# The split products of a two-model transformer kernel with their moving operand and their PSUM columns taken in descending order

## What is computed

```
h = modulate(x, g_norm1, sh1, sc1)
proj = h @ w_in                                  # 1024 x 5024
y = g_mla*(o_mla @ w_br_mla) + g_gqa*(o_gqa @ w_br_gqa) + g_four*(o_four @ w_four)
x = x + gt1 * (y @ w_o)
u = modulate(x, g_norm2, sh2, sc2) @ w_up        # 1024 x 5632
u = conv3(u) + conv_b
a, v = split(u, 2); x = x + gt2 * ((silu(a) * v) @ w_down)
...
gate, up = split(x @ wi, 2); x = x + (silu(gate) * up) @ wo
```

## Time and profile before

| | |
|---|---|
| median of 3 runs | 2618.41 us (2617.87 to 2620.92) |
| span of the profiled execution | 2618.2 us |
| PE busy | 2498.0 us, 95% |
| PEld busy | 2204.9 us, 84% |
| DVE busy | 1609.7 us, 61% |
| ACT busy | 1333.9 us, 51% |
| POOL busy | 585.6 us, 22% |
| mean granted TensorE clock | 0.985 of full |
| HBM traffic | 171 GB/s |

### The profile page before, as it was taken

The page is one execution under the profiler, slowest core; times in us unless marked ns, Lnnn a source line. Parts: engine busy times, 40 slices in busy tenths (PEclk is TensorE's granted clock), DMA queues, the critical chain, the costliest instruction groups (busy, mean ns, idle before and its releaser), DMA issues. The chain is left out here.

```text
span 2618.2 us, 46369 instructions
## 1 busy us (share of the span) xinstructions
PE 2498.0 (95%) x17358; PEld 2204.9 (84%) x17358; DVE 1609.7 (61%) x2387; ACT 1333.9 (51%) x2155; POOL 585.6 (22%) x429
## 2 busy tenths in 40 slices
PE   6999999999899998999999999997999999989998
PEld 5876899888599988876899899886998899758986
DVE  3654777566477757774777466545665654556545
ACT  3434566454547644535477454444554554455544
POOL 1110333221022321101233232020231232112311
PEclk9999999999999999999999999998999999989999
DMA  8565555556245655464455566562466466524663
GB/s 282 179 227 192 153 177 185 166 184 197 77 136 173 186 164 159 151 223 160 153 178 184 192 203 197 161 210 76 130 193 194 153 196 191 170 80 141 188 200 122
DMA packets 332945, 450.54 MB, mean 172 GB/s; under 512 B 28192, under 2 KB 207392, under 8 KB 332768
## 3 DMA queue, kind: packets, MB, share of 16 engines
q1 hardware_dynamic: 332400, 446.58, 54.2%
q0 software_dynamic: 368, 1.57, 0.2%
HBM read 446.99 MB, written 1.05 MB: 171 GB/s over the span
## 5 line engine op out<-in xcount | busy, mean ns | idle before, releaser
L744 DVE TENSOR_TENSOR wlo<-raw,whi 128x1024 fp32r<-128x1024 f32 (+4 forms) x631 | 806.6, 1291 | 657.8 <-ACT whi L738 652.6
L738 ACT CAST whi<-raw 128x1024 fp32r<-128x1024 f32 (+2 forms) x776 | 768.3, 1006 | 664.5 <-PE S L1041 238.3
L1057 PE MATMUL S<-hhi,whi 128*128 128x256 f32 x1952 | 546.6, 280 | 4.0 <-DVE wlo L744 2.5
L1057 PE MATMUL S<-hlo,whi 128*128 128x256 f32 x1952 | 544.4, 279 | 1.2 <-DVE hlo L1966 1.1
L1057 PE MATMUL S<-hhi,wlo 128*128 128x256 f32 x1952 | 544.5, 279 | 0.0
L744 POOL TENSOR_TENSOR wlo<-raw,whi 128x1024 fp32r<-128x1024 f32 (+3 forms) x145 | 338.4, 2334 | 708.6 <-ACT whi L738 707.6
L1057 PEld LDWEIGHTS S<-hhi,whi 128*128 128x128 f32 x1952 | 366.4, 188 | 5.6 <-issue 4.0
L1057 PEld LDWEIGHTS S<-hlo,whi 128*128 128x128 f32 x1952 | 366.5, 188 | 1.8 <-DVE hlo L1966 1.7
L1057 PEld LDWEIGHTS S<-hhi,wlo 128*128 128x128 f32 x1952 | 366.4, 188 | 0.0
L1057 PE MATMUL G<-hhi,whi 128*128 128x256 f32 x1088 | 305.4, 281 | 0.7 <-ACT hhi L1412 0.4
L1057 PE MATMUL G<-hlo,whi 128*128 128x256 f32 x1088 | 302.2, 280 | 0.1
(11 more groups left out here) (372 smaller groups left out, 4450.6 us busy)
## 6 DMA issues: line engine op xcount, KB each, us to landing
raw<-in_ffn_wi SPq DMA_DIRECT2D x352, 256.0 KB, 3.5
raw<-in_w_up SPq DMA_DIRECT2D x264, 256.0 KB, 3.5
modw<-in_w_mod SPq DMA_DIRECT2D x192, 256.0 KB, 4.8
raw<-in_w_in SPq DMA_DIRECT2D x192, 256.0 KB, 3.0
raw<-in_ffn_wo SPq DMA_DIRECT2D x160, 256.0 KB, 3.5
raw<-in_w_down SPq DMA_DIRECT2D x120, 256.0 KB, 3.3
raw<-in_a_wqkv SPq DMA_DIRECT2D x72, 256.0 KB, 3.0
raw<-in_w_o SPq DMA_DIRECT2D x48, 256.0 KB, 3.2
```

What stands on the lines that cost most here:

```text
L738: act.copy(whi[:, n0 % SPLIT, z, w], raw[:, n0 % RAW, z, w]).then_inc(hi_done, 1)
L744: eng.tensor_tensor(wlo[:, n0 % SPLIT, z, w], raw[:, n0 % RAW, z, w], whi[:, n0 % SPLIT, z, w].bitcast(F32), ALU.subtract)\
L1057: mm = pe.matmul(out_[:, m * T:(m + 1) * T], w, x, start=first and c == 0 and m == 0 and z == 0, stop=last and c == kc - 1 and z == len(te ...
```

## The change

Both matmuls in `passes` get `[:, ::-1]` on the moving operand and on the output. The moving operand is read from its last column to its first, with a step of -1 element, and the PSUM columns are written in the same descending order, so each column of the result stands where it stood. The stationary operand, the instructions, their order and every wait are as before: each engine's list has the same rows (11,519 written-out rows on PE). In the compiled program the moving operands and outputs of `passes` have step -1 in place of 1, at 256, 288, 384 and 512 columns.

```
-mm = pe.matmul(out_[:, 0:n], x, w, start=first and c == 0 and z == 0,
+mm = pe.matmul(out_[:, 0:n][:, ::-1], x, w[:, ::-1], start=first and c == 0 and z == 0,
                stop=last and c == kc - 1 and z == 2, skip_group_check=True)
...
-mm = pe.matmul(out_[:, m * T:(m + 1) * T], w, x, start=first and c == 0 and m == 0 and z == 0,
+mm = pe.matmul(out_[:, m * T:(m + 1) * T][:, ::-1], w, x[:, ::-1], start=first and c == 0 and m == 0 and z == 0,
                stop=last and c == kc - 1 and z == len(terms) - 1, skip_group_check=True)
```

## The result

The changed kernel takes 2658.7 us (median of 4), the kernel before 2619.4 us beside it (median of 4): ratio 1.0156, 95% interval 1.0143 to 1.0168. It is slower by about 40 us; I had forecast no change at 2618 us, with 0.44 for slower. The profiled executions differ by 39.5 us (2657.7 against 2618.2 us), the granted clock is 0.985 in both.

The account below looks back on a forecast made before the run. The prediction took PE's matmul pace as the bound and summed the change as 14,100 matmuls x 0 = 0, giving 2618 us; the range was 2600 to 4420 us.

Parts of the forecast that it names:

- What bounds the kernel: PE sets the pace, busy 2498.0 of 2618.2 us; lines 1057 and 1041 together cover 2092 us, 80%.
- Nothing: Lines 1057 and 1041: descending column order costs no time, 14,100 x 0 = 0; the term taken.
- A few ns per instruction: Rival for lines 1057 and 1041: for example a longer start per product, 5 ns each, 71 us, 2689 us; chance 0.14.
- Half pace or worse: Rival for lines 1057 and 1041: descending columns cannot pair into one access, 1745 us more, 4365 us; chance 0.30.
- A part of the surplus goes: Rival for lines 1057 and 1041: time above one column per cycle shrinks, 2482 us at most, 2550 for half; chance 0.13.
- the lower bound: Lines 1057 and 1041: time above one column per cycle cut to 1 to 2 ns, gaining 136 us, 2482 us.
- the likeliest case: Lines 1057 and 1041 keep their pace: 2618 us, own range 2612 to 2624; chance 0.43.

Follow-up runs that it names:

- step2_read: Kernel before, with the moving operand of both lines read even columns first, then odd, and PSUM written upwards (result columns permuted): 4560.9 us.
- write_down: Kernel before, with only the PSUM columns written downwards and the moving operand still read upwards: 2618.2 us, ratio 1.0005.
- shift48: Kernel before with SHIFT 48 instead of 16, placing `hhi`, `hlo` and two `b_o` tiles 128 bytes higher: 2604.2 us against 2617.1, ratio 0.9959.
- up_w64: Kernel before, still reading upwards, with table `den` allocated behind `whi` and `wlo` so these lie 64 bytes lower: 2647.3 us, one run.

## Why the prediction was wrong, point by point

- **What bounds the kernel** was right: PE's pace passed one to one into the time (42.7 us in the two lines, 39.5 in the span), no other engine moved, and half pace passed whole as well (step2_read: the two lines cover 2283.03 and 1761.93 us, 1952.8 more than before, and the span grew by 1940.6).
- **"Nothing", the term that I took** (14,100 x 0), is the step that failed: it measured 9,984 x 2.4 ns and 3,192 x 6.3 ns, all of it on the reading side. I gave as reasons the same pairs, the same distance of revisits and the same count. They hold for PSUM, where write_down shows 1.0005, and neighbours that stay neighbours kept the half pace away. But they leave out that the pace of the read depends on where the moving operand lies to the stationary one, and on the order in which its 64-byte pieces come. The sentence that the feeding "is tolerant only to a few per cent of loss either way, for which I have no sign" was wrong in its second half; the earlier trace rows had the same shape at 118 and 113 ns, and the `hhi` rows of line 1041 at 233 ns beside 227 were in the same trace.
- **A few ns per instruction**, a rival with 0.14, was the right kind, and its condition ("which operand comes from where is worth 5 ns") the right sign. Mis-sized: 14,100 x 5 = 71 us, where line 1057 lost 2.4 ns and line 1041 6.3, together 43. Line 1057 was already half out of tune at 117.6 and had less to lose to the 120.0 that both directions have as their worst. That the price is by the instruction was right: between the best and the worst pace seen lie 6.5 ns at 256 columns (113.5 in a stretch of shift48, 120.0) and 6.3 at 512 (227.1, 233.4), not twice as much at 512. Its mechanism, a longer start of a descending read, is refuted for line 1057, which regains 117.8 to 118.4 ns at four placements, and it does not explain up_w64, where an ascending read pays. For the descending read of line 1041 it is not refuted.
- **Half pace or worse**, to which I gave 0.30, did not come; the condition that I had named, two columns not sharing one access, fits step2_read, on the reading side, though a step of -1 does not meet it. The Trainium skill's rule in "PSUM — Partial Sum Buffer", Specifications (TRN2), that any non-contiguous pattern slows matmuls significantly, does not hold for a descending write of all columns: 227.1 ns, ratio 1.0005. What the Trainium skill's page "Advanced Engine Details and Errata", Memory Cachelines, wants of SBUF, two hits on a 16-byte line, is not enough: step2_read has two hits on each and runs at half pace.
- **A part of the surplus goes** came in neither direction of the walk. But the lower bound had its point: a stretch of shift48 runs at 113.5 ns. The surplus of one cycle in 16 itself I found in every kernel at the full clock, and nothing removed it.
- **The range** ran from 2600 to 4420 us and held the time; the likeliest case was the wrong one. That the range held the time is no merit of the sum, since it had been widened for the half pace.

What is shown: the price is of reading; it comes with the order of the 64-byte pieces; an ascending read pays the same price in line 1041 when the weight tiles move by 64 bytes; the place of the stationary tile counts as well; in line 1057 a descending read regains 118 ns by placement. What is only argued: that it is the read of the next product's stationary operand that the moving read meets. What stays open: why line 1041 at 512 columns found no good place for a descending read at 0, 32, 64, 96, 128 or 192 bytes, so that I can't say whether one exists or whether direction has a price of its own there. A kernel without the stationary reads was not tried.

## What to carry to other kernels

In a kernel whose matmuls run back to back at one column per cycle, read the distance of starts by tile name, not by shape alone: two groups of one shape at 227 and 233 ns can be a matter of where the operands lie, which can be set; here one constant gained 0.4%, in the line with 256 columns. A step of -1 through the whole operand did not bring the half pace, only 2 to 3% of a product's time, and PSUM may be written in descending order for free, but any change in how an operand is walked has to be tuned for its placement anew. Avoid steps of two columns in a 4-byte moving operand, which cost half the pace, and an order in which pieces of 16 columns go up and the columns within them down, which cost this kernel 11%.

## What the runs showed of the hardware that I had not expected

- Placement of the two operands in SBUF, in steps of 32 or 64 bytes, moves the pace of fp32r products that read upwards between 115.6 and 120.0 ns (256 columns) and between 227.1 and 233.4 ns (512), in both cases at the full clock.
- At the lower clock the descending read costs nothing: 214 ns for 256 columns, 213.3 before.
- Reading and writing each 16 columns downwards while the blocks go upwards takes 1.67 ns a block above one column per cycle, 133.3 and 266.7 ns; reading and writing the blocks downwards and the columns in them upwards costs 120.0 and 233.4 ns.
- A moving operand in steps of two 4-byte columns runs at 228.0 and 451.9 ns, twice the unit-step pace with its surplus.
- PSUM written in descending order costs nothing, ratio 1.0005 (0.9991 to 1.0019).
